# Sample attention directly behind the prompt, and one joint merge for prompt tiles 1 to 3 and the sample tokens

## The reference

```python
z = x @ w_in      # q, k, v of DSA and FoX heads, indexer q, k, w, forget logits, two gates
# DSA, 8 heads on 2 kv heads: scores of an indexer, top-k keys per query, softmax over those
I = einsum('bqh,bqhs->bqs', w_i, relu(einsum('bqhd,bsd->bqhs', q_i, k_i))) * IDX_SCALE
# FoX, 8 heads: softmax(q.k / sqrt(d) + sum of log f between the key and the query)
h = LN1(ALPHA * x + w_out(sigmoid(g_a) * (y_a @ w_branch_a) + sigmoid(g_b) * (y_b @ w_branch_b)))
# PEER: 8 heads x 16 experts per token, out of 16384, found by product keys
y = LN2(ALPHA * h + sum over the 128 experts of gate * peer_v[e] * gelu(peer_u[e] . h))
```

## Time and profile before

| | |
|---|---|
| time, median of 3 runs | 2402.66 us (2399.91 to 2403.54) |
| span of the profiled execution | 2493.9 us; no separate time is given for it |
| PE, DVE, POOL busy | 1810.2 us (73%), 1433.9 (57%), 1307.8 (52%) |
| DMA moved | 791.92 MB, mean 318 GB/s |
| gathers (software queue) | 604.58 MB, 63.6% of 16 engines' span |
| SyncE's transfers (hardware queue) | 180.82 MB, 20.6% |
| first gather issued | 439.1 us |

### The profile page before, as it was taken

One profiled execution on the slowest core, in us unless ns is written; L12 is line 12 of the kernel. 1 busy time (PEld: TensorE's weight loads), 2 busy tenths in 40 slices (PEclk: granted clock), 3 DMA queues, 4 the chain that ended last, 5 costly groups with the idle time before them and its releaser, 6 DMA issues.

```text
span 2493.9 us, 23573 instructions
## 1 busy us (share of the span) xinstructions
PE 1810.2 (73%) x7244; PEld 768.0 (31%) x7247; DVE 1433.9 (57%) x3191; ACT 307.8 (12%) x732; POOL 1307.8 (52%) x1175
## 2 busy tenths in 40 slices
PE   9999988899699635566666766776777884555566
PEld 6767646644244201111112121221223250110011
DVE  2115876898845643999856569854444437434400
ACT  0214442111011101001101010110110010000000
POOL 1100000467655744555555557766777747677664
PEclk9998987999899867777778789998999997876678
DMA  5206322999989976999999999999999999999997
GB/s 182 71 3 195 102 85 68 355 328 410 361 306 368 346 281 238 394 367 400 386 401 380 401 371 362 371 356 368 378 384 409 409 370 374 364 359 380 355 377 287
DMA packets 259648, 791.92 MB, mean 318 GB/s; under 512 B 31522, under 2 KB 56163, under 8 KB 258947
## 3 DMA queue, kind: packets, MB, share of 16 engines
q0 software_dynamic: 166400, 604.58, 63.6%
q1 hardware_dynamic: 91268, 180.82, 20.6%
q10 hardware_dynamic: 1856, 5.03, 0.5%
HBM read 784.13 MB, written 5.59 MB: 317 GB/s over the span
## 4 chain that ended last, share of the span: by engine, by line
POOL 13%; DMA 10%; PE 8%; issue 7%; SPq 7%; another core or an unknown queue 6%; DVE 2%; ACT 1%; POOLq 0%
POOL arena L918 13%; DMA arena<-v_b 4%; PE ps L1369 3%; SPq L841 3%; DMA arena<-peer_v,arena 3%; SPq L768 2%; DMA arena<-peer_u,arena 2%; PE ps L1325 2%; DMA arena<-kv_a 2%; SPq L834 1%; PE ps L1202 1%; DVE arena L2081 1%; PE ps L1302 1%; ACT arena L1640 0%
## 5 line engine op out<-in xcount | busy, mean ns | idle before, releaser
L1369 PE MATMUL ps<-arena 128*32 128x512 f32 x2304 | 767.5, 717 | 346.6 <-DMA arena<-peer_v,arena 287.9
L2081 DVE CUSTOM_DVE_ANT_0 arena<-arena 128x1024 f32<-128x1024 f32 x576 | 694.7, 1225 | 531.5 <-DMA arena<-peer_u,arena 475.7
L918 POOL DMA_INDIRECT arena<-peer_v,arena x576 | 623.4, 1082 | 445.9 <-PE ps L1369 245.0
L918 POOL DMA_INDIRECT arena<-peer_u,arena x576 | 664.1, 1153 | 311.8 <-issue 162.2
L1369 PEld LDWEIGHTS ps<-arena 128*32 128x32 f32 x2304 | 153.4, 122 | 877.7 <-issue 662.1
L1164 PE MATMUL ps<-arena 128*128 128x448 f32 (+2 forms) x512 | 156.8, 467 | 13.1 <-DVE arena L1997 12.4
L1202 PE MATMUL ps<-arena 128*128 128x384 f32 (+2 forms) x704 | 146.5, 368 | 10.0 <-ACT arena L1576 8.1
L1325 PE MATMUL ps<-arena 128*64 128x512 f32 (+1 forms) x512 | 102.6, 538 | 68.1 <-DMA arena<-v_b 57.3
L900 POOL MEMSET arena<- 128x1024 f32 x1 | 1.0, 953 | 282.4 <-ACTq L723 282.4
L950 PE MATMUL ps<-arena 128*128 128x296 f32 (+1 forms) x512 | 132.1, 419 | 6.2 <-DMA arena<-xT 6.2
L1699 ACT ACTIVATE arena<-arena 128x8 f32<-128x8 f32 x72 | 15.3, 216 | 943.1 <-PE ps L1369 635.2
(11 more groups left out here) (211 smaller groups left out, 1694.1 us busy)
## 6 DMA issues: line engine op xcount, KB each, us to landing
arena<-k_b SPq DMA_DIRECT2D x128, 256.0 KB
arena<-v_b SPq DMA_DIRECT2D x128, 256.0 KB
arena<-w_mix SPq DMA_DIRECT2D x56, 512.0 KB
arena<-w_q SPq DMA_DIRECT2D x48, 512.0 KB
arena<-kv_a SPq DMA_DIRECT2D x128, 128.0 KB
arena<-w_out SPq DMA_DIRECT2D x24, 512.0 KB
arena<-peer_u,arena POOLq DMA_INDIRECT x576
arena<-peer_v,arena POOLq DMA_INDIRECT x576
```

The costliest lines, as they stand in the source:

```text
L918: pool.indirect_dma_start(out=rows[slot_of[n]], out_offset=None, in_=io["peer_v"] if v else io["peer_u"], in_offset=bass.IndirectOffsetOnA ...
L1369: last = pe.matmul(bank(6 + a, 512, 32 * lane, 32 * lane + 32), strips[:, GT * (G % 2) + k % GT, MID - r_:MID - r_ + 32], rows[slot_of[n]] ...
L2081: dve.tensor_tensor_reduce(out=row, in0=row, in1=h, scale=1.0, scalar=0.0, op0=ALU.mult, op1=ALU.add, accum_out=pre[:, k:k + 1]).then_inc( ...
```

## The change

- Sample attention is planned from n = 4, directly behind the last queries of tile 0, with smaller gaps, scaled by 0.65.
- The second merge takes prompt tiles 1 to 3 and the sample tokens together, 448 columns wide (`REST`), with gaps scaled by 0.75; the third merge goes. The sample tokens' attention results are written into the last 64 columns of `yaT` and `ybT`. The output product has still two parts: tiles 1 to 3, and tile 4, which takes tile 1's banks once its residual is read (`OUT_TILES`, `OUT_BANK`).
- SyncE's order is `first_queries()`, `sample()`, `second_merge()`, `pack_last()`: x rows, norms and the second sub-key load move behind the sample attention.
- The index pages no longer wait for tile 1's key scores, but the last group of them for tile 0's.
- The gather list weaves `peer_v` of tile i - 1 with `peer_u` of tile i, with 64 `peer_v` gathers of tile 3 alone behind tile 4's `peer_u`; value rows that aren't four in a row are summed in pairs.
- The page ring, `hrow[4]` and others get other places; the 16 gather slots come from `SWITCH`, now behind tile 4's key scores.

```diff
-        later = vs[1] + vs[2] + vs[3]
         ALONE = 72
-        gathers = us[0] + vs[0][:ALONE] + weave(us[1], vs[0][ALONE:]) + weave(us[2], later[:120]) + weave(us[3], later[120:244]) + later[244:320]
-        gathers += weave(us[4], later[320:370]) + later[370:] + vs[4]
+        gathers = us[0] + vs[0][:ALONE] + weave(us[1], vs[0][ALONE:]) + weave(us[2], vs[1]) + weave(us[3], vs[2]) + weave(us[4], vs[3][:64])
+        gathers += vs[3][64:] + vs[4]
...
-                size = 4 if span == 3 else 2 if gather_at[i, 1, k] > gather_at[4, 0, 0] - 130 else 1
+                size = 4 if span == 3 else 2
...
-            out = [(("zero",), 0), (("spread", 0), 1), (("ix", 0), 3), (("iy", 0), 34), (("ix", 1), 12)]
+            out = [(("zero",), 0), (("spread", 0), 1), (("ix", 0), 1), (("iy", 0), 6), (("ix", 1), 4)]
             for c in range(2, 5):
-                out += [(("ix", c), 2), (("iy", c - 1), 14 if c == 2 else 3)]
-            out += [(("iy", 4), 2), (("admit",), 1)]
-            out += [(("s_score", 0, c), 5) for c in range(5)]
-            out += [(("s_max", 0), 2), (("s_exp", 0), 2), (("s_norm", 0), 2), (("s_turn", 0), 3)]
+                out += [(("ix", c), 1), (("iy", c - 1), 6 if c < 4 else 1)]
+            out += [(("iy", 4), 1), (("admit",), 1)]
+            out += [(("s_score", 0, c), 1) for c in range(5)]
+            out += [(("s_max", 0), 1), (("s_exp", 0), 1), (("s_norm", 0), 1), (("s_turn", 0), 1)]
...
+        SAMPLE_PACE, MERGE_PACE = 0.65, 0.75
+        at = 4
         q_at_ = {}
         for item, gap in sample_items():
             put(at, *item)
-            q_at_[item[:2]] = at
-            at += gap
-        s_end = at
-        top_from, top_to = q_at_[("admit",)] + 2, q_at_[("s_out", 3)] + 24
+            q_at_[item[:2]] = int(at)
+            at += SAMPLE_PACE * gap
+        s_end = int(at)
+        top_from, top_to = q_at_[("admit",)] + 1, q_at_[("s_out", 3)] + 1
...
+        at = s_end + 2
+        for item, gap in merge_items(1):
             put(at, *item)
-            at += gap
-        m4_end = at
-        SWITCH = -(-(s_end + 24) // NR0) * NR0
+            at += MERGE_PACE * gap
...
+        for g in range(4):
+            put(where["gate", 1] + 2 + g, "score", 4, g)
+        SWITCH = -(-(where["score", 4, 3] + 24) // NR0) * NR0
...
+            def second_merge():
+                sp.wait_ge(se_ready, NB)
+                for i in range(1, 5):
+                    if i == 4:
+                        sp.wait_ge(se_done, NB)
+                    x_rows(i)
+                sp.dma_start(lng, io["ln"][0:1, :].partition_broadcast(128)).then_inc(ln_loaded, 16)
+                sp.dma_start(lnb, io["ln"][1:2, :].partition_broadcast(128)).then_inc(ln_loaded, 16)
+                sp.dma_start(subk[:], io["subk"]).then_inc(subk_loaded, 16)
+                for w in range(first_mix + NMW, len(merge_weights)):
+                    weights(w)
+                sp.wait_ge(ln1_done, 5)
...
                 for c in range(4):
-                    if c:
-                        sp.wait_ge(sc_ready, 13 + c)
-                    else:
-                        sp.wait_ge(mix_done, KD)
+                    if c == 3:
+                        sp.wait_ge(sc_ready, 4)
...
             end_phase(sp, 2)
-            first_merges()
+            first_queries()
             sample()
-            last_merge()
+            second_merge()
             pack_last()
...
-                if m == 0 and p == 1:
+                if m == 0:
                     pe.wait_ge(sc_copied, 4)
                     pe.wait_ge(qp_copied, 2 * PH)
-                if m == 0 and p == 2:
                     pe.wait_ge(se_done, NB)
```

More of the change, by code:

```diff
@@ L289, in program @@
         b_at = r.at
-        hT_all = r.take(KD, 384)
+        hT_all = r.take(KD, REST)
         subk = r.take(2 * PH, 128)
-        sig = [r.take(384) for _ in range(2)]
+        sig = [r.take(REST) for _ in range(2)]
         assert r.at <= b_end, (r.at, b_end)
@@ L295, in program @@
         mw_k = [w.rearrange("p (k n) -> p k n", k=KD) for w in mw]
[L297 to L301, removed]
-        MIX_IN = [(xT[:, :, 16:144], yaT[:, :, 0:128], ybT[:, :, 0:128]),
[L303 to L309, removed]
+        hT = [hT_0, hT_all]
+        qpT = [Region(sc_at + 4096).take(2 * PH, 128), Region(a_at, a_end).take(2 * PH, REST)]
+        MIX_IN = [(xT[:, :, 16:144], yaT[:, :, 0:128], ybT[:, :, 0:128]),
+                  (xT[:, :, 144:T], yaT[:, :, 128:], ybT[:, :, 128:])]
+        PASS = ((0,), (1, 2, 3, 4))
+        WIDTH = (128, REST)
+        PASS_OF = (0, 1, 1, 1, 1)
+        OUT_OF = (0, 1, 1, 1, 2)
+        OUT_TILES = ((0,), (1, 2, 3), (4,))
+        OUT_BANK = (0, 0, 2, 4, 0)
         NSLOT = 4
-        ring = [r.take(2048) for _ in range(NSLOT)]
-        ring = ring[3:] + ring[:3]
+        r = Region(a_end, sc_at)
+        ring = [r.take(2048) for _ in range(2)]
         osb = r.take(512)
-        relu_s = [Region(ya4_at).take(512), osb]
+        relu_s = [r.take(512), osb]
+        r = Region(sc_at + 2048, sc_at + 3 * 2048)
+        ring += [r.take(2048) for _ in range(NSLOT - 2)]
         r = Region(b_at, b_end)
@@ L498, in merge_items @@
         def merge_items(p):
-            out, tiles = [], PASS[p]
+            out = []
             if p:
-                out += [(("mix", p, 0), (0, 10, 6)[p])]
+                out += [(("mix", 1, 0), 5)]
                 for m in range(1, KD):
[L503 to L506, removed]
@@ L507, in merge_items @@
-            out += [(("turn", i), 2 if i == 3 else 1) for i in tiles]
+                    out += [(("mix", 1, m), 2), (("mixed", 1, m - 1), 3)]
+                out += [(("mixed", 1, KD - 1), 1)]
+                out += [(("out", 1, k), 2) for k in range(KD)]
+                out += [(("norm", i), 1) for i in (1, 2, 3)]
+                out += [(("out", 2, k), 0) for k in range(KD)] + [(("norm", 4), 1)]
+            out += [(("turn", i), 1) for i in PASS[p]]
             for m in range(2 * PH):
-                out.append((("query", p, m), (2, 4, 1)[p]))
+                out.append((("query", p, m), (2, 2)[p]))
@@ L510, in merge_items @@
                 if m % 4 == 1 and m > 4:
[L511 to L513 removed]
+                    out.append((("score", PASS[p][0], m // 4 - 1), 1))
+            out += [(("score", PASS[p][0], 3), 1)]
+            out += [(("score", i, g), 1) for i in PASS[p][1:3] for g in range(4)]
             return out
         def sample_items():
[L517 removed]
+            out = [(("zero",), 0), (("spread", 0), 1), (("ix", 0), 1), (("iy", 0), 6), (("ix", 1), 4)]
@@ L547, in program @@
         put(42, "gate", 0)
-        at = 0
-        for item, gap in merge_items(1):
-            put(at, *item)
-            at += gap
-        m1_end = at
-        for g in range(4):
-            for s_ in range(4):
-                put(where["score", 1, g] + 2 + 3 * s_, "route", 1, g, s_)
-        put(where["route", 1, 3, 3] + 2, "gate_in", 1)
-        put(where["route", 1, 3, 3] + 5, "gate", 1)
-        at = s_start = m1_end + 2
+        SAMPLE_PACE, MERGE_PACE = 0.65, 0.75
+        at = 4
         q_at_ = {}
@@ L583, in program @@
             put(at + 88, "gate", i)
+        assert where["score", 4, 3] > where["gate", 1]
         for i in range(5):
@@ L590, in program @@
                 put(max(n + (3 if last else 14), 47 if i == 0 else 0), "coefs", i, g)
-        bank4 = [(where["mix", p, m], where["mixed", p, m]) for p in (1, 2) for m in range(KD)]
+        bank4 = [(where["mix", 1, m], where["mixed", 1, m]) for m in range(KD)]
         bank4 += [(where["s_score", q, 4], where["s_exp", q]) for q in range(NB)]
```

148 lines of the change are left out of this document (64 added, 84 removed).

## The result

The changed kernel takes 2848.57 us (median of 4 runs, 2844.06 to 2852.90), the kernel before 2401.28 (4 runs, 2398.26 to 2403.54). The ratio is 1.1858, 95% interval 1.1819 to 1.1897: 447 us slower. 2840 was forecast, in a range of 2660 to 2970.

A forecast was written before the change was run, and what follows sets the result against it. The DMA engines bound the kernel before; after the change, SyncE's issue would pace the sample block and PE the merge. 1192 + 372 + 1364 + 20 = 2948 us profiled, times 0.963 gives 2840; range 2660 to 2970.

The forecast's parts named there:

- Index pages: Start of sample attention: SyncE issues 128 transfers of 32 KB in 190 us, from 465 to 655; stall costs about 150.
- First scores: After the index pages: four k pairs of 8 us, landing and scores, 43 us.
- FoX periods: Sample queries 0 to 3: 78 us each, 17 of chain, the rest pages; DVE's 52 lies under it.
- DSA periods: Sample queries 4 to 7: page issue in series with scores, landing and chain, 52 us each.
- Sample block: Sample attention behind tile 0: index pages, first scores, FoX and DSA parts, weighings and output, ending at 1192 us.
- Merge: Joint merge of tiles 1 to 3 and sample tokens: 372 us, set by PE, tile 4's output product covered.
- Gather 200: First gather row of tile 1, issued at 1564 us after sample block and merge; it was 825 before.
- Rest: Gathers 200 to 1151: 951 intervals at 1.434 us each, 1364 us.
- the conversion: Whole sum of 2948 us in profile time scaled by 0.963, median over profiled span, to 2840 us.
- Issue hidden: Rival: SyncE's issue is hidden and engines pace the sample block, 419 us; total 2543 us, chance 0.12.
- Faster: Rival: the DMA stays full and fewer bytes move, total 2311 us; chance 0.04.
- More waiting: Rival: slower page landing, late DVE or slower PE clock add waits, total 3014 us; chance 0.12.

The follow-up runs named there:

- the three index runs: Changed kernel, index pages as 32 transfers of 128 KB from fixed pages (2863.47 us), 128 without reading page numbers (2774.03), or 256 of 16 KB (2894.51).
- wide pages: Changed kernel with index pages as 32 transfers of 128 KB and FoX and DSA pages as one 1 MB transfer a fill, from fixed pages: 2806.53 us.
- the kernel before with wide index pages: Kernel before with the index pages as 32 transfers of 128 KB from fixed pages instead of 128 of 32 KB: 2398.53 us, ratio 0.9982.
- the kernel without issue and selection: Changed kernel with all sample pages by one transfer a fill (32 for the index pages), from fixed pages, and no top-8 rounds: 2685.38 us, ratio 1.116.

## Why the prediction was right

Measured beside predicted, all in the changed kernel's profile:

- *Index pages.* 190 us to 655 were forecast; it was 145.6 to 603.3. The mechanism held: SyncE's own issue, as the three index runs show. The term was mis-sized by 44 us. The prediction took the two equal rows of 43.3 for SyncE's own pace; that is 35 a quarter, and both rows had been stretched. Another 7 us are the earlier start. By the rule that a sequencer's time is "usually small relative to the DMA itself" (the Trainium skill, DMA: Bandwidth & Descriptors, section "Issuing engines are not separate DMA queues") the prediction's estimate was 11 us; the changed kernel's trace disagrees as well, with 145.6.
- *First scores*: 43 forecast, 603.3 to 646.7, 43. With wide pages they still take 45, so issue is not all that they need.
- *FoX periods*: 78 forecast, 86, 87 and 79 measured. Of the 78, 61 were pages at SyncE's pace, and 60 to 64 were measured: right, with the ring's round trip close below (57 without issue). The step that failed is the chain: 17 forecast, 26.2, 23.6 and 16.8 measured, because DVE's written order puts the top-8 rounds into it, which the prediction held to be covered. No single part gives more than 16 us of a period when it is taken away.
- *DSA periods*: 52 forecast, 48 measured; 41 to 44 with wide pages, so these edits take some 6 off.
- *Sample block*: forecast to end at 1192, ended at 1133.2. Of the 59 us, 44 are the index row and 7 its earlier start; the DSA part and the weighings at its ends took 26 less than forecast, and the three FoX periods 19 more.
- *Merge*: 372 forecast, 377 measured. A 448-wide record takes 98.8 / 256 = 0.386 us (0.381 forecast). Tile 4's output product runs at 1323.75 for 14.0 us, and behind it PE waits another 3.9 us for DVE's norms (shown above), so it is covered, as forecast.
- *Gather 200*: 1564 forecast, 1510.3.
- *Rest*: 1364 forecast, 1306.5, at 1.374 us an interval for 1.434. In the predicted units of the median, 1364 x 0.963 = 1314. *End*: 20 forecast, 25.
- *Rates*: forecast 270, 180, 230 and 368 GB/s for FoX, DSA, merge and rest; measured 275, 207, 205, and 375 to 405.

**The step that was wrong although the sum came out** is the conversion. 2948 is 3.7% above the span that was measured. The factor 0.963 was put on all of it; it stands for a quicker chip, and belongs only to what the DMA bounds, which is the rest (1314 against 1306.5). On the sample block and the merge, which wait for engines and issue, the chip gives nothing; there the factor took off 58 us of 1564 (1506) and so hid the 54 that the terms were too long. Two errors of opposite sign and nearly equal size: that the centre came within 0.3% of the time is luck. The range and the mechanism of the stall are not.

**Where the 447 us are.** Against the kernel before with wide index pages, which takes the same time as the kernel before and ran on an equally quick chip: gather 200 is at 1510.3 and not at 819.5, 691 later. Behind it the same 951 intervals take 1306.5 and not 2370.3 - 819.5 = 1550.8 us, 244 less, because no sample page and no third merge lies beside them (606 MB moved there, 500 here). 691 - 244 = 447, the difference of the two medians. Before tile 1 has routed there are 200 gathers in all, 260 us of DMA at 1.3 us each, beside 1053 us of sample block and merge. In the order before, 562 gathers were at hand for the sample block alone. The 13.6 MB saved (778.2 MB after, 791.9 before) are in the 244 as far as they lay there.

**The rivals.** *Issue hidden* (2543): no, and even the kernel without issue and selection takes 2685, since the round trip and the chain remain. *Faster*: the sample block had to last under 273 us; it lasts 676, and 519 in the best run. *More waiting*: no; gather 200 came before the forecast, not behind it. A version that beats both kernels was not pointed to by any of the runs.

**Open.** What stretches the 128 issues by 8 to 48 us in the kernel before and never in the changed one. What sets the two kinds of chip apart. What a ring of more pairs, with SyncE's issue as it is, would give in the FoX periods.

## What to carry to other kernels

Before a block is moved ahead of others, count what the dependencies still let run beside it there: its own time hardly changes, but the work that used to hide it may not exist yet. An engine that issues transfers in order, with page numbers read into registers, is a resource with a price for each transfer that doesn't follow its bytes (0.65 us for 32 KB and 0.46 for 1 MB here, both without page numbers), and its price shows as soon as nothing else is in flight. Take the size of such a row from several executions, and don't take two equal rows of one trace for an engine's own pace. What an engine does between two links of a chain belongs to the chain, even where its total fits under another engine's time. Where a limit is taken away, look what its engine waits for instead. Convert between two chips only the part of the sum that the chip's difference touches.

## What was not expected of the hardware

- The chips are of two kinds for this kernel: 1.42 to 1.44 us against 1.26 to 1.28 us for a gather of 0.524 MB at the end, and 2472 to 2482 against 2400 to 2407 us for the whole. Stretches that wait for SyncE, PE or DVE don't show it.
- 128 transfers of 32 KB take SyncE 83.6 us to issue, and reading their 128 page numbers in 32 groups, with the addresses made from them, another 62 us, 1.9 a group. The row takes 145.5 to 145.7 us in four executions of the changed kernel and its variants, on both kinds of chip, and 153.6 to 193.9 in four of the kernel before and its variant. A second transfer for a page whose number is in a register takes 0.35 us.
- In a loop of a chain (17 to 26 us) and a stretch with two limits of nearly one length (issue 60 to 64, ring 57 to 58), taking away SyncE's issue gave 5 us a period, half the bytes 4 to 6, the top-8 rounds 1 to 16, and the first and third together 13 of 84.
